# Dividing by the root mean square at the eviction of a projection instead of in front of it, in a three-block model on one core

## The reference

```
# first model
u = rms_norm(h, norm_mix);  proj = u @ w_in          # 20 tiles of 128 features, and 8 columns a, b
mix = [ pooled windows @ w_pool , gated_delta_net(conv+silu(q,k,v), z, a, b) ]   # q, k l2-normed
h = h + mix @ w_out
u = rms_norm(h, norm_mlp);  h = h + square(relu(u @ w_up)) @ w_down
h = rms_norm(h, norm_final)
# second model, layer 0: compressed + causal attention, silu(z) gate; layer 1: S5 state space, glu
h = h + nsa_mixer(rms_norm(h, l0_norm))
h = h + s5_mixer(rms_norm(h, l1_norm))
out = rms_norm(h, final_norm)
# rms_norm(x, w) = x * rsqrt(mean(x*x) + 1e-6) * w, over the 1024 features of a token
```

## Time and profile before

| | |
|---|---|
| time, median of 3 runs | 1534.01 us (1532.36 to 1534.39) |
| the profiled execution: its time, its span | 1536.8 us, 1535.0 us |
| PE busy | 1368.0 us, 89% |
| PE weight load | 1059.6 us, 69% |
| DVE busy | 814.4 us, 53% |
| ACT busy | 438.7 us, 29% |
| POOL busy | 908.5 us, 59% |
| mean granted TensorE clock | 0.956 |

### The profile page before, as it was taken

One profiled execution on the slowest core, in us unless ns is written; L12 is line 12 of the kernel. 1 busy time (PEld: TensorE's weight loads), 2 busy tenths in 40 slices (PEclk: granted clock), 3 DMA queues, 4 the chain that ended last, 5 costly groups with the idle time before them and its releaser, 6 DMA issues.

```text
span 1535.0 us, 23038 instructions
## 1 busy us (share of the span) xinstructions
PE 1368.0 (89%) x8212; PEld 1059.6 (69%) x8212; DVE 814.4 (53%) x1386; ACT 438.7 (29%) x816; POOL 908.5 (59%) x704
## 2 busy tenths in 40 slices
PE   4979768797999899998959999988898979999986
PEld 2758668684887678887827878745555858878874
DVE  3754797414999921176032904368875136842312
ACT  3025620304321113300051112277765041331102
POOL 3859401073999988899627982900000837658962
PEclk9989978999999999999979999999999989999999
DMA  4213100023332443335717330300001519733321
GB/s 149 69 55 90 55 1 3 7 76 80 97 95 76 171 135 106 96 105 150 232 36 212 96 96 21 97 1 1 2 1 41 206 56 213 221 117 94 97 77 62
DMA packets 86048, 137.95 MB, mean 90 GB/s; under 512 B 16464, under 2 KB 34384, under 8 KB 84816
## 3 DMA queue, kind: packets, MB, share of 16 engines
q1 hardware_dynamic: 48384, 88.10, 19.5%
q10 hardware_dynamic: 37584, 48.71, 10.0%
HBM read 119.02 MB, written 20.91 MB: 91 GB/s over the span
## 4 chain that ended last, share of the span: by engine, by line
PE 74%; DVE 11%; issue 5%; POOL 5%; ACT 4%; DMA 1%; DVEq 0%; ACTq 0%; POOLq 0%
PE ps L353 18%; PE ps L355 18%; PE ps L354 18%; POOL wh L1178 4%; PE ps L346 3%; PE ps L661 3%; PE ps L673 2%; PE ps L650 2%; DVE xs L1245 2%; DVE uL L1235 1%; PE ps L494 1%; PE ps L731 1%; DVE bigB L1675 1%; PE ps L599 1%; DVE bigB L1355 1%
## 5 line engine op out<-in xcount | busy, mean ns | idle before, releaser
L1178 POOL TENSOR_TENSOR wh<-raw,small 128x512 fp32r<-128x512 f32 x336 | 413.4, 1230 | 347.6 <-PE ps L355 336.9
L1180 POOL TENSOR_TENSOR wl<-raw,wh 128x512 fp32r<-128x512 f32 x336 | 482.1, 1435 | 26.3
L353 PE MATMUL ps<-uH,wh 128*128 128x512 f32 x800 | 323.2, 404 | 33.8 <-DVE uL L1235 33.6
L354 PE MATMUL ps<-uL,wh 128*128 128x512 f32 x800 | 317.7, 397 | 0.0
L355 PE MATMUL ps<-uH,wl 128*128 128x512 f32 x800 | 317.3, 397 | 0.0
L353 PEld LDWEIGHTS ps<-uH,wh 128*128 128x128 f32 x800 | 153.7, 192 | 80.1 <-issue 27.7
L355 PEld LDWEIGHTS ps<-uH,wl 128*128 128x128 f32 x800 | 154.0, 193 | 33.0
L354 PEld LDWEIGHTS ps<-uL,wh 128*128 128x128 f32 x800 | 154.2, 193 | 31.0 <-issue 0.5
L353 PE MATMUL ps<-ffH,wh 128*128 128x512 f32 x256 | 102.7, 401 | 17.0 <-POOL wl L1180 16.8
L354 PE MATMUL ps<-ffL,wh 128*128 128x512 f32 x256 | 99.9, 390 | 0.0
L355 PE MATMUL ps<-ffH,wl 128*128 128x512 f32 x256 | 99.8, 390 | 0.0
(11 more groups left out here) (346 smaller groups left out, 2284.5 us busy)
## 6 DMA issues: line engine op xcount, KB each, us to landing
raw<-wstream SPq DMA_DIRECT2D x336, 256.0 KB, 2.6
b_powers_scratch<-bigB ACTq DMA_DIRECT2D x4, 1024.0 KB, 4.8
c_powers_scratch<-bigB ACTq DMA_DIRECT2D x8, 512.0 KB, 4.8
lags_scratch<-lag_rows_scratch ACTq DMA_DIRECT2D x8, 512.0 KB, 7.6
bigB<-b_powers_scratch ACTq DMA_DIRECT2D x4, 1024.0 KB, 8.2
bigB<-lags_scratch ACTq DMA_DIRECT2D x4, 1024.0 KB, 6.7
bigB<-c_powers_scratch ACTq DMA_DIRECT2D x4, 1024.0 KB, 9.5
hT<-x ACTq DMA_DIRECT2D x1, 2048.0 KB, 8.9
```

Source lines behind the costliest of these rows:

```text
L353: pe.matmul(out, lh, rh, start=first, stop=False)
L354: pe.matmul(out, lh, rl, start=False, stop=False)
L1178: pool.tensor_tensor(wh[:, j, :], raw[:, j, :], zero_ap.to_broadcast([128, 512]), ALU.add).then_inc(half_lead, 1)
L1180: pool.tensor_tensor(wl[:, j, :], raw[:, j, :], wh[:, j, :].bitcast(f32), ALU.subtract).then_inc(half_split, 1)
```

## The change

Since rms(h) is one factor for each token, that is for each column, `(h*w*r) @ W = ((h*w) @ W) * r`. The projections now take h*w, and r is multiplied in where a bank is evicted.

- **Inputs.** As soon as a tile of hT has its residual, ACT copies hT*w into `uH` (`weigh_lead`) and squares the tile; DVE forms `uL` in one instruction (`weigh_rest`) and adds the square to `acc` (`add_square`). PE sums `acc` with one matmul (two for norms 2 and 3) after the first tile of the next projection (`between`, `sum_squares`); ACT forms the root (`root`).
- **Evictions.** "inp", "nsa", "zed" and tiles 0 to 7 of "sin" are evicted by DVE as bank * rms. Silu of z follows on ACT in place. z of "sin" is copied out by ACT and scaled by DVE (`scale_z`). "up" is evicted without r; the residuals of "down" first multiply the bank by r*r in PSUM. "val" is scaled by ACT with r turned onto the partitions (`rcol`).
- **Norms 2 and 3** become one: both sums are taken from the same tiles, and the input is h*(norm_final*l0_norm). hT itself is normed by `block_output` between evictions of "nsa".
- **Start.** x is loaded in four pieces behind the parameters.
- **inp.** The order on PE is now: tiles 0 to 3, a and b, 4, 5, transposes, 6, 7, pooling, 8, 9, gate sums, 10, 11, `l2_sums(0, 4)`, 12 to 14, `l2_sums(4, 8)`, 15, 16, the row sums of the decays, 17, 18, round "attn", 19, round "attnT". The convolution's first tap is ACT's (`leading_tap`).
- **Order under the new norms.** ACT issues `store_c`, decays and `store_lags` between the tiles of "down1". In "nsa" DVE evicts 0 to 3, norms `hT` 0 to 3, evicts 4, norms 4 to 7, evicts 5, waits for `swapped_in`, and then for each of 8 groups makes four of the additions and evicts one tile (6 to 13). In "sin" the eviction of u is DVE's, `evict_u(7)` behind `chunk_states(1)`, and ACT's `store_u(3)` waits for it, with `load_b(3)`, `evict_y(0)`, `load_y(1)` and `evict_z(8)` behind.
- **Buffers.** `acc` is new; "sin" reads `sH`, `sL` in the place of nsT; u and z of "sin" lie in uT and mixT; `qdec` has another place, with a wait for it. POOL splits the gates' weights behind "val" instead of ahead of "nsa".

```diff
+            def sum_squares(n):
+                pe.wait_ge(sq_added, SQUARES[n])
+                for i in range(2 if n == 2 else 1):
+                    j = pe.matmul(ps[:, 4 + i, :], ones, acc[:, i, :], start=True, stop=True)
+                j.then_inc(rms_sum, 1)
...
+            inp_tile(0)
             pe.wait_ge(s_const, 16)
-            rms_pe(0)
-            tile_group("inp", 0, u_parts, first=True, ready=(rms_out, 0))
+            sum_squares(0)
+            for n in range(1, 4):
+                inp_tile(n)
...
-            linear("up0", ready=(rms_out, KT))
+            linear("up0", ready=(g_split, KT), between=lambda: sum_squares(1))
-            rms_pe(2)
-            rms_pe(3)
-            linear("nsa", ready=(rms_out, 3 * KT))
+            linear("nsa", ready=(g_split, 2 * KT), between=lambda: sum_squares(2))
...
-            for n in range(5):
+            in_tile(0)
+            sum_squares(3)
+            for n in range(1, 5):
                 in_tile(n)
+            pe.wait_ge(r_ready, 5)
             chunk_inputs(0)
...
             linear("sout", x=(mH, mL))
-            rms_pe(5)
+            sum_squares(4)
+            def weigh_lead(k, dst, weight):
+                act.activation(dst[:, k, :], hT[:, k, :], ACT.Copy, scale=weight[:, k:k + 1]).then_inc(g_lead, 1)
+            def square(n, k):
+                if n == 2:
+                    if k >= 2:
+                        act.wait_ge(sq_added, squares_before(n) + 2 * (k - 1))
...
+            def root(n, power):
+                act.wait_ge(rms_sum, n + 1)
+                own(act.activation(rms[:, :], ps[:, 4, :], ACT.Ln, scale=1.0 / D, bias=eps_ap))
+                act.activation(rms[:, :], rms[:, :], ACT.Exp, scale=power).then_inc(r_ready, 1)
+            def residual_tile(n, name, k, dst=None, weight=None):
+                act.wait_ge(tile_evicted, TILE0[name] + k + 1)
+                if dst is not None:
+                    weigh_lead(k, dst, weight)
+                square(n, k)
...
-            evict_in(7)
             store_u(3)
             load_b(3)
             evict_y(0)
             load_y(1)
-            evict_in(8)
+            evict_z(8)
...
+            def weigh_rest(k, dst, leading, weight, count):
+                dve.wait_ge(g_lead, count + 1)
+                dve.scalar_tensor_tensor(dst[:, k, :], hT[:, k, :], weight[:, k:k + 1], leading[:, k, :].bitcast(f32),
+                                         ALU.mult, ALU.subtract).then_inc(g_split, 1)
+            def add_square(n, k):
...
+                    dve.tensor_tensor(acc[:, i, :], acc[:, i, :], xs[:, i if n == 2 else k % 2, :], ALU.add).then_inc(sq_added, 1)
+            def add_tile(name, n, scaled=False):
...
+                if scaled:
+                    own(dve.tensor_tensor(ps[:, n % 4, :], ps[:, n % 4, :], rms[:, :], ALU.mult))
+                dve.tensor_tensor(hT[:, n, :], hT[:, n, :], ps[:, n % 4, :], ALU.add).then_inc(tile_evicted, 1)
+            def residual(name, n, rest):
+                for k in range(KT):
+                    add_tile(name, k)
+                    if k:
+                        rest(k - 1)
+                rest(KT - 1)
+            def evict_inp(n):
+                dve.wait_ge(half_used, 2 * n + 2)
+                dve.tensor_tensor(projT[:, n, PAD:PW], ps[:, n % 4, :], rms[:, :], ALU.mult).then_inc(tile_evicted, 1)
...
+            for n in range(5):
+                evict_u(n)
             chunk_states(0)
+            evict_u(5)
+            evict_u(6)
             chunk_states(1)
+            evict_u(7)
             skip(0)
             chunk_states(2)
```

More of the change, by code:

```diff
@@ L283, in build @@
         y_lead = sem("y_lead")
-        s_x = sem("x_loaded")
+        s_x = [sem(f"x_{k}_loaded") for k in range(KT // 2)]
         s_const = sem("consts_loaded")
@@ L575, in _ @@
             down(1, {t: lambda c=c: lag_kernel(c) for c, t in enumerate((1, 2, 3, 5))})
-            rms_pe(2)
-            rms_pe(3)
-            linear("nsa", ready=(rms_out, 3 * KT))
+            linear("nsa", ready=(g_split, 2 * KT), between=lambda: sum_squares(2))
+            pe.wait_ge(r_ready, 4)
+            for tt in range(TT):
+                i = pe.matmul(ps[:, 4, tt:tt + 1], rms[0:1, tt * 128:(tt + 1) * 128], ones[0:1, 0:1], start=True, stop=True)
+            i.then_inc(rcol_mm, 1)
             pe.wait_ge(tile_evicted, TILE0["val"])
@@ L972, in _ @@
                         act.activation(ffH[:, m * 4 + j, :], squared[:, j, :], ACT.Copy).then_inc(ff_lead, 1)
-            for c in range(4):
-                store_c(c)
-            act.wait_ge(rho_done, 1)
-            act.dma_start(scratch["decays"], rho0.rearrange("p g c -> p (g c)")).then_inc(rho_stored, 16)
-            store_lags()
+            act.wait_ge(zero_stored, 16)
+            act.wait_ge(w_both, 1)
+            for k in range(KT):
+                if k < 4:
+                    store_c(k)
+                if k == 5:
+                    act.wait_ge(rho_done, 1)
+                    act.dma_start(scratch["decays"], rho0.rearrange("p g c -> p (g c)")).then_inc(rho_stored, 16)
+                if k == 6:
+                    store_lags()
+                residual_tile(2, "down1", k, uH, both_w)
+            act.wait_ge(rms_sum, 3)
+            act.wait_ge(eps_mixed, 1)
+            act.activation(acc[:, 0, :], ps[:, 4, :], ACT.Ln, scale=1.0 / D, bias=eps_ap)
+            own(act.activation(rms[:, :], rms[:, :], ACT.Ln, scale=1.0 / D, bias=eps2_ap))
+            act.activation(rms[:, :], rms[:, :], ACT.Exp, scale=-0.5).then_inc(r_ready, 1)
+            act.activation(acc[:, 0, :], acc[:, 0, :], ACT.Exp, scale=-0.5).then_inc(r_ready, 1)
             act.wait_ge(b_stored, 4 * 16)
@@ L985, in _ @@
             act.dma_start(w_gate, A["w_gate"]).then_inc(s_wgate, 16)
-            act.wait_ge(tile_evicted, TILE0["down1"] + 8)
-            rms_act(2)
-            act.wait_ge(rms_out, 3 * KT)
-            rms_act(3)
-            for k in range(KT):
-                lead(uH[:, k, :])
             spread_lags()
-            evict("nsa", 0, 4, lambda n, p: act.activation(nsT[:, 8 + n, :], p, ACT.Copy))
             act.wait_ge(tile_evicted, TILE0["nsa"] + 4)
@@ L1665, in _ @@
                 dve.tensor_tensor(pc[tt], pc[tt], wide(cs_), ALU.mult).then_inc(cs_p, 1)
+                evict_zed(tt + 1)
+            for n in range(TT + 1, 8):
+                evict_zed(n)
+            dve.wait_ge(zs_gated, 8)
             def shift(u):
@@ L1792, in _ @@
                 dve.wait_ge(glu_o, m * 2 + 2)
-            residual("sout")
-            rms_dve(5, "final_norm", hT)
+            residual("sout", 4, lambda k: add_square(4, k) if k else None)
+            dve.wait_ge(r_ready, 6)
+            dve.wait_ge(tile_evicted, NTILE)
+            for k in range(KT):
+                dve.scalar_tensor_tensor(hT[:, k, :], hT[:, k, :], param("final_norm")[:, k:k + 1], rms[:, :],
+                                         ALU.mult, ALU.mult).then_inc(rms_out, 1)
 def constants():
```

497 lines of the change are left out of this document (319 added, 178 removed).

## The result

The changed kernel takes 1445.6 us in the median (1442.7 to 1453.9, four runs), the kernel before 1534.2: a ratio of 0.943 (0.939 to 0.947). The prediction said 1446 in a range of 1424 to 1472.

The account below looks back on a forecast made before the run. TensorE, with 74% of the chain, was taken as the bound. Gains 34 + 17.5 - 3 + 24 + 10 + 5 = 87.5 us gave 1534 - 88 = 1446 us, 8-in-10 range 1424 to 1472.

Parts of the forecast that it names:

- A: Start to round "attnT": the round begins at 162 instead of 196.24, a gain of 34 us.
- rms is there at 27: First stage: 15 two-operand DVE instructions end at about 23; sum and root add 4 us.
- Neither has slack: First stage: PE passes tile 18 and DVE finishes its list at the same date, 146 us.
- B: "out" to end of "down0": PE gains 19.5 us, but DVE's tables limit the gain to 17.5, bounds 15 and 20.
- down1: Stage "down1": added two-operand DVE work beside `powers_of_c` slows GpSimd, 7 x 0.4 us; taken as -3, bounds -1 and -6.
- C: "down1" to "val": copies of swapped halves queue behind w1 and the lags, landing at E+55; gain 24 us, bounds 20 and 35.
- PE waiting for evictions of nsa tiles 6 to 13: Expected sign in "nsa": these evictions stand in DVE's list of groups, so PE waits for DVE; no size given.
- Rival 1: Queues don't bite: copies land early and `evict_y(0)` is not late; gains 35 and 19.5 us, 1425 us; chance 0.13.
- D: "nout" to "glu": 19.5 us from the early tile, less 7.7 at y(0) and 2.5 for y(1)'s load; gain 10.
- E: Last residual to the norm of hT at the end: 10.55 us becomes 5.4 to 6, a gain of 5.
- Rival 2: DVE and GpSimd bound "inp", two-operand instructions stretching both: 12 to 24 us more, about 1465 us; chance 0.2.
- Rival 4: GpSimd becomes the bound in stages with new DVE work, from a mean half of 3.24 us; slower; chance 0.03.

Follow-up runs that it names:

- root_first: Changed kernel with the sum of squares and the wait for the root ahead of the first tile at up0, nsa and sin; 1468.4 us, ratio 0.9572.
- two_taps: Changed kernel with the first of DVE's three taps of each convolution working on only 2 columns; 1442.2 us in one run.

## Why the prediction was right, and where its steps were not

**A (34 said, 33.6 measured): right by errors that cancelled.** The first product came at 9.5 and not at 11.6. "rms is there at 27" was 32.6: the 15 two-operand instructions ended at 26.4 and not 23 (1.35 us for each `weigh_rest`, and additions and squares take turns in a ring of two buffers), the sum and the root took 6.2 us and not 4, and PE, which has nothing else to do then, waited 7.1 us that no term held. PE passed tile 18 at 151.7, not 146. The terms given for it add up to 11.6 + 103 + 20 + 3 = 137.6 and not to 146, so the sum for PE was 14 us short, and the prediction's 146 rests on DVE's list alone. What made up for it: the exponentials of the decays ran beside tiles 17 and 18 (145.9 to 153.9), where the sum had put them behind. "Neither has slack" was wrong for DVE: the profile shows it idle in front of evictions, and a shorter list moved the stage by 0.4 us. And the pooling's wait wasn't closed by the order of tiles.

**B (17.5 said, 17.6 measured): size right, limit wrong.** The sum took the smaller gain because "down0" was to wait for DVE's tables. Delaying PE alone lengthened B by 10.7 us, though the tables were then earlier and not later, and leaving out the 16 scaling instructions changed nothing: PE, fed by GpSimd, sets the stage. Its gain can be followed. The first product of tile 1 of "up0" came 8.6 us behind the last residual (7.3 said) against 25.9, that of tile 2 at 14.1 against 32.0, and these 18.0 us stayed up to the end of "up0"; that ACT reached the first relu only behind the root (331.3) cost PE nothing. The waits of PE in B, the changed kernel and then the kernel before, show the rest:

```profile
PE ps L373 <- POOL wl L1281: 9.0, 10, 1.2
PE ps L373 <- DVE ffL L1730: 3.2, 5, 0.7
```
```profile
PE ps L353 <- POOL wl L1180: 12.1, 12, 1.3
```

The wait for DVE's tables that the sum feared is there, 3.2 us at the turn to "down0", and 3.1 us less waiting for GpSimd made up for it.

**down1 (-3 said, +0.3 measured).** The additions beside `powers_of_c` cost DVE time but hardly PE's: with them shortened it was 1.4 us less, against the 2.8 counted. What takes up the rest wasn't tried.

**C (24 said, 28.3 measured): mechanism right, two sizes off.** The copies landed 56 us behind the last residual (said: 55). But the hold-up showed at the lags' issue, 24 us for eight instead of 12, more than at the landing. The DVE list behind it took 44.3 us up to "val" and not 49.5: a group with its eviction came every 5.4 to 5.6 us from 784 on, not every 6.1, so its four additions cost less than the 5.40 of the earlier trace rows; why, no run shows. Of the sign "PE waiting for evictions of nsa tiles 6 to 13" the profile has one wait of 2.4 us; the other, 4.1 us, stands at "val". Rival 1, that the queue doesn't bite, is excluded: without the hold-up C is 93.5. The Trainium skill, DMA: Bandwidth & Descriptors, Queues, rings and completion order, has descriptors consumed in ring order on each DMA engine. The trace of the changed kernel agrees as to the order: the loads of w1, w2 and the gates had landed at 745.1, the lags landed from 747.1 to 762.3 and the copies from 762.3 to 769.1. That the issues themselves were held, no term had.

**D (10 said, 9.0 measured): right, with its wait.** 6.9 us at the turn of y(0) against 7.7 said, ended by ACT. PE was 19.0 us ahead up to the turn (19.5 said) and 9.7 behind it: besides the wait it lost 2.4 us at a granted clock of 0.81 in the 15 us from 1216 on, where the kernel before had 1.00. So the 2.5 counted for the late load of y(1) had the right size and the wrong reason: that load was covered by the wait and came out at 6.3 once it was gone.

**E (5 said, 4.1 measured)**, mostly from a shorter sum; two table loads of 1.28 us stay in it. **Rival 2** fell: its 12 to 24 us didn't come, and a list of DVE shorter by 6.7 us moved the stage by 0.4. **Rival 4** fell: GpSimd's half was 3.1 us beside short instructions in the stretch shown, and 4.48 beside the tables, as before. The 3.3 us between round "attnT" and the last residual of "out" no term held, and rightly: they are the granted clock of that execution, 0.94 against 0.89.

## What to carry to other kernels

A factor that is constant along the contraction can leave the input of a projection and be applied at the eviction. At the three norms where it was parted, 26 of 55 us came from the norm standing beside the first tile, so look for what stands there with it. An instruction that moves from one engine to another moves every transfer queued behind its semaphore: go through the in-order queue that waits for it, and past the first wait to the next. When a predicted total comes true, check the stretches one by one: here terms were right for the wrong reason, 3 us were the clock of one execution, and 21 us of the median lay in two orders that cost nothing to change.

## What the runs showed of the hardware

A two-operand instruction of DVE that starts while GpSimd has one under way costs up to a microsecond more, however short it is. The timeline of the changed kernel has the same instruction on 2 columns with GpSimd at work, and on 8 columns while it stood idle:

```profile
36.30 1.36 POOL L1281 TENSOR_TENSOR wl<-raw,wh 128x512 fp32r<-128x512 f32 x1
36.54 1.13 DVE L1394 TENSOR_TENSOR bigB<-bigB,const_table 128x2 f32<-128x2 f32 x1
...
50.86 0.17 DVE L1394 TENSOR_TENSOR bigB<-bigB,const_table 128x8 f32<-128x8 f32 x1
```

1.13 against 0.17: DVE's instruction ended at 37.67, with that of GpSimd (37.66). The wait is for the instruction that GpSimd has under way, not a share of bandwidth. The Trainium skill, SBUF — State Buffer, Who interferes with whom, calls it an exclusive lock for the whole instruction, and this row agrees. It isn't two-operand instructions alone: L1393 with one operand of 512 columns took 1.15 us at 35.36 beside GpSimd and 0.43 at 50.40 without. Nor does each one pay. Of the 32 instructions on 32 columns with which the tables begin (320.99 to 355.84) 18 took less than 0.5 us and 14 more; in `root_first`, where GpSimd was at work for 3.4 us of it, 29 and 3, and the same list took 17.2 us instead of 34.9. So such a list is counted by its number, and by how much of it GpSimd is at work. A DMA issue isn't a fixed price: eight issues of 512 KB took 24 us of ACT's queue with 4.3 MB in flight ahead of them and 12.5 to 14.2 without. And the granted clock differs between executions of the same code where PE has many short pauses: 0.89 to 0.94 ahead of "out", worth 4 us, and 0.92 to 1.00 in the attention part, worth some 7 us (331.5 us in `two_taps` against 338.9, both with the wait ahead of "val"). What decides it no run here shows.
